# Output products started inside the merge stage, casts moved to ScalarE, wider bank rotation, short token tile last

## The chip, the cores and the metric

The kernel runs on one core of a Trainium2 chip. The metric is the device time in microseconds of one execution, the median of several runs. TensorE multiplies, VectorE and ScalarE do elementwise work, GpSimd (POOL in the profile) does a few fills, and SyncE (SP) issues the loads and stores.

## The reference

One inference step of a one-layer decoder, for a prompt of 512 tokens and 8 single-token samples, 520 tokens in all, model width 1024. What matters here is the end of the layer:

```
merged = (gates[:, :, 0] * einsum(o_nsa, w_br_nsa)
          + gates[:, :, 1] * einsum(o_gdn, w_br_gdn)
          + gates[:, :, 2] * einsum(o_mem, w_br_mem))
h = x + einsum('btd,de->bte', merged, w_out)
f = square(relu(einsum(rmsnorm(h, g_ffn), w_ff1)))
y = h + einsum('btf,fd->btd', f, w_ff2)
```

The gates are sigmoids of a projection of the normalized input. Everything is fp32.

## The kernel before

The program is six stages, each a block that all engines leave together. The last two are concerned: `stage_tail` (gates, branch projections, merge) and `stage_out_ffn` (output projection, norm, MLP). Between two stages local semaphores are cleared and all engines meet at a barrier.

**Precision.** Each fp32 operand x is split into a high part (a cast to fp32r) and a low part (x minus high), and each product is made of three matmuls per 128-row chunk: high x high, high x low, low x high (`product3`, L330). The cast is L299 and the subtraction L301, both in the helper `high_low` on VectorE, for weight tiles and activations alike. The low part is written over its source.

**Merge stage.** Weights come in tiles of 256 columns. The list `seq` alternates gate tiles (8 chunks, 24 matmuls a unit) and branch tiles (4 chunks, 12 matmuls a unit): gate 0, gate 1, then branch q and gate q + 2 for q = 0 to 11; the last two tiles are branches 10 and 11. A tile has four units: two blocks of 128 output columns times two halves of 260 tokens. TensorE writes gate units to banks 0 and 1 and branch units to banks 2, 3 and 4, and a branch unit waits until VectorE has taken the product three units back (`taken`). ScalarE makes the sigmoid (L2633). VectorE multiplies branch by gate (L2698), adds into `mergedT` (L2700) and, in the last third (branches 8 to 11, units 32 to 47), splits the finished unit into `mergedH` and the low part (L299, L301). The order on each engine is written out by `by_key`: small generators yield a due time, and the instruction with the lowest key is issued next. After `split(n)` of the next weight tile come the four units of a branch on VectorE; the last weight tile handled there, number 24, is the first tile of `w_out`.

**Output stage.** There are 20 output products, one for each of 5 token tiles (four of 128 rows, t = 0 to 3, and one of 8 rows, t = 4) and 4 column tiles n of `w_out`: first n = 0 for all t, then n = 1 for all t (products 0 to 9), then for each t in `order` n = 2 and n = 3 (10 to 19). Product u goes to bank 4 + u % 4 and waits, from u = 4 on, for the addition to h of product u - 4 (`h_ready`). h starts as x, loaded by SyncE at the start of the stage (2 MB, L2856). VectorE's order is: split of `w_out` tile 1 (`last_raw`), split of tile 2, five additions of n = 0, split of tile 3, five additions of n = 1, and so on. The loads of tiles 2 and 3 are also issued at the start of the stage. For each t in `order`, ScalarE sums squares (L2971), takes the root (L2980) and scales the rows (L2984), TensorE transposes them (`norm_turn`, L2901), and VectorE multiplies by the gain (L3010) and splits (`norm_keep`). The MLP's first unit needs the first three token tiles and its third unit needs all five. GpSimd fills `yT` with zeros once the last transposes are done (L2882). The MLP is four quarters of 32 units of 24 matmuls.

Of the kernel before, what the change touches and what calls it, by code (L numbers as in the profile page):

```python
# [169 lines left out]
class Kernel:  # L170
# [2238 lines left out]
    def tile_units(self):  # L2409

        return [(m, slice(HALF * h, HALF * h + HALF)) for m in range(WM) for h in range(2)]

    def out_tiles(self):
        return [[self.I["w_out"][:, a:a + WCOLS]] for a in range(0, DM, WCOLS)]

    def stage_tail(self):
# [67 lines left out]
        S = self.local_sem  # L2484
        gated, taken, added = (S("m_" + x) for x in ("gated", "taken", "added"))
        turned, oH_kept, oL_kept = (S("t_" + x) for x in ("turned", "oH_kept", "oL_kept"))
# [9 lines left out]
        with nc.Block() as block:  # L2496
# [44 lines left out]
            def _(pe):  # L2541
# [77 lines left out]

                by_key(dense(), turn(), sample())  # L2620

            @block.scalar
            def _(act):
                def dense():
                    for n, (kind, q) in enumerate(seq):
                        if kind == "gate":
                            for i, (m, tok) in enumerate(U):
                                yield unit_at(n, i + 1)
                                u = NU * q + i
                                act.wait_ge(acc, acc_of("gate", q, i))  # L2630
                                if q >= 2:
                                    act.wait_ge(taken, u - 2 * NU + 1)
                                act.activation(sig[:, q % 2, m, tok], ps[:, u % 2, 0:HALF], ACT.Sigmoid).then_inc(gated, 1)  # L2633
# [23 lines left out]

                by_key(dense(), turn(), sample())

            @block.vector  # L2660
            def _(dve):
                ch = Chain(S("s_chain"), dve)

                def split(n):
                    k, chunks = k0 + n, tiles[n][1]
                    dve.wait_ge(self.w_loaded[k % 2], self.loaded_at[k])
                    if n >= 2:
                        dve.wait_ge(acc, self.tile_end[k - 2])
                    cut = lambda x: x[:, 0:chunks, :]
                    self.high_low(dve, cut(raw[n % 3]), cut(self.wh[k % 2]), cut(low[n % 3]), self.w_high, k + 1).then_inc(self.w_split, 1)  # L2670

                def splits():
                    yield 0.1
                    split(0)
                    for n in range(1, NT_ + 1):
                        yield start[n - 1] + 0.2
                        split(n)

                def dense():
                    for n, (kind, q) in enumerate(seq):  # L2680
                        if kind == "gate":
                            continue
                        for i, (m, tok) in enumerate(U):
                            yield unit_at(n, i + 1) + 0.1
                            u = NU * q + i
                            dst, high, lo = (x[:, WM * (q % BP) + m, tok] for x in (self.mergedT, self.mergedH, self.mergedL))
                            dve.wait_ge(gated, u + 1)
                            dve.wait_ge(acc, acc_of("branch", q, i))
                            if u == 0:
                                dve.wait_ge(turned, EARLY)  # L2690
                            x, y = ps[:, 2 + u % 3, 0:HALF], sig[:, q % 2, m, tok]
                            if q < BP:
                                dve.tensor_tensor(dst, x, y, ALU.mult).then_inc(taken, 1)
                                continue
                            e = u - BP * NU
                            if e >= 2:
                                dve.wait_ge(added, e - 1)
                            dve.tensor_tensor(prod2[:, e % 2, :], x, y, ALU.mult).then_inc(taken, 1)  # L2698
                            dve.wait_ge(taken, u + 1)
                            dve.tensor_tensor(dst, dst, prod2[:, e % 2, :], ALU.add).then_inc(added, 1)  # L2700
                            if q >= 2 * BP:
                                dve.wait_ge(added, e + 1)
                                self.split_acts(dve, dst, high, lo)

# [97 lines left out]
    def stage_out_ffn(self):  # L2802
# [24 lines left out]
        acc, u0 = self.acc, self.units  # L2827
        order, UN, NO = (0, 1, 2, 4, 3), TT + 1, DM // WCOLS
        token = lambda t: slice(t * P, t * P + rows(t))
# [23 lines left out]
        with nc.Block() as block:  # L2853
# [31 lines left out]
            def _(pe):  # L2885
                def out_product(n, t):
                    u = index[n, t]
                    w = (self.wh[(base + n) % 2], wlow[(base + n) % 2]) if n < 2 else (woH[n - 2], woL[n - 2])
                    pe.wait_ge(self.w_split, base + n + 1)
                    if u >= 4:  # L2890
                        pe.wait_ge(h_ready, u - 3)
                    self.product3(pe, ps[0:rows(t), 4 + u % 4, 0:WCOLS], lambda i, c: X[i][:, c, token(t)], lambda i, c: w[i][:, c, :]).then_inc(acc, 1)

# [10 lines left out]
                for n in range(2):  # L2904
                    for t in range(UN):
                        out_product(n, t)
# [84 lines left out]
            def _(dve):  # L2991
# [6 lines left out]
                def add(n, t):  # L2998
                    R, u = rows(t), index[n, t]
                    hh = h[0:R, t, WCOLS * n:WCOLS * n + WCOLS]  # L3000
                    dve.wait_ge(acc, u0 + u + 1)
                    dve.tensor_tensor(hh, hh, ps[0:R, 4 + u % 4, 0:WCOLS], ALU.add).then_inc(h_ready, 1)  # L3002

# [16 lines left out]
                dve.wait_ge(h_in, 32)  # L3020
                for n in range(2):
                    split_out(n + 2)
                    for t in range(UN):
                        add(n, t)
                for k, t in enumerate(order):
# [97 lines left out]
```

## Time and profile before

| | |
|---|---|
| time, median of 3 runs | 1560.75 us (1556.61 to 1567.21) |
| profiled execution, its own time | 1570.02 us |
| its span | 1568.2 us |
| TensorE busy | 1434.7 us, 91% |
| VectorE busy | 865.2 us, 55% |
| ScalarE busy | 391.2 us, 25% |
| mean granted TensorE clock | 0.945 |

The span runs from the first to the last instruction; the execution's own time is 1.8 us longer. In the trace's rows a time is in microseconds from the start of the span, a matmul's own duration includes its passage through a pipeline, so the distance between starts is its cost, and the brackets at a row's end hold how long the engine was idle before it and what released it.

### The profile page before, as it was taken

The numbers are of one execution on the slowest core, as the hardware profiler recorded it, in microseconds if no ns is written. First come the engines' busy times: TensorE is split into PE (matmuls) and PEld (weight loads), VectorE is DVE, ScalarE is ACT, GpSimd is POOL, SyncE is SP. The second block draws the span as 40 slices with busy tenths as digits, with TensorE's granted clock in tenths as the row PEclk, the third lists the DMA queues.
The fourth block names the chain that finished last, engine by engine and source line by source line (L and its number), as shares of the span: only waits on it lengthen the run. The fifth ranks groups of instructions, "written<-read, shape, count | busy, mean of one in ns | idle before, by whom it ended". The sixth has DMA issues, their size and how long they took to land. (4 is left out here: it accounts for less than half of the span.)

```text
span 1568.2 us, 27050 instructions
## 1 busy us (share of the span) xinstructions
PE 1434.7 (91%) x11344; PEld 1322.1 (84%) x11344; DVE 865.2 (55%) x1576; ACT 391.2 (25%) x895; POOL 79.7 (5%) x74
## 2 busy tenths in 40 slices
PE   6999999999887887889667899999799999999998
PEld 5888889899877776768444798999799999999998
DVE  3556257877463665554524545545647647465563
ACT  3543032332352444443313410000021001010000
POOL 1000001100011111111000000000000000000000
PEclk8999999999988897979879899999999999999999
DMA  9132134222432000010666413332521232323221
GB/s 361 66 137 102 39 92 175 81 81 85 129 131 108 1 1 1 1 54 1 224 263 252 141 56 109 106 108 68 174 69 55 94 95 81 108 80 96 93 81 55
DMA packets 115648, 159.03 MB, mean 101 GB/s; under 512 B 6039, under 2 KB 106839, under 8 KB 112778
## 3 DMA queue, kind: packets, MB, share of 16 engines
q1 hardware_dynamic: 111886, 122.76, 24.5%
q0 software_dynamic: 2304, 33.56, 5.4%
q8 instruction: 84, 1.38, 0.4%
q10 hardware_dynamic: 1348, 1.12, 0.2%
q14 instruction: 26, 0.21, 0.0%
HBM read 145.04 MB, written 16.66 MB: 103 GB/s over the span
## 5 line engine op out<-in xcount | busy, mean ns | idle before, releaser
L330 PE MATMUL ps<-hH,wh 128*128 128x260 f32 x512 | 146.3, 286 | 2.6 <-DVE hT L301 2.6
L330 PE MATMUL ps<-hT,wh 128*128 128x260 f32 x512 | 146.0, 285 | 0.0
L330 PE MATMUL ps<-hH,wl 128*128 128x260 f32 x512 | 145.7, 285 | 0.0
L330 PE MATMUL ps<-mergedH,wh 128*128 128x260 f32 x512 | 145.7, 285 | 0.0
L330 PE MATMUL ps<-mergedT,wh 128*128 128x260 f32 x512 | 144.8, 283 | 0.0
L330 PE MATMUL ps<-mergedH,wl 128*128 128x260 f32 x512 | 144.5, 282 | 0.0
L330 PE MATMUL ps<-uH,wh 128*128 128x260 f32 x480 | 138.2, 288 | 0.0
L462 PE MATMUL ps<-XT,w 128*128 128x256 f32 (+1 forms) x512 | 124.3, 385 | 0.3 <-DVE hbias L615 0.3
L330 PE MATMUL ps<-uL,wh 128*128 128x260 f32 x384 | 109.4, 285 | 0.0
L330 PE MATMUL ps<-uH,tw 128*128 128x260 f32 x384 | 109.4, 285 | 0.0
L462 PEld LDWEIGHTS ps<-XT,w 128*128 128x128 f32 x512 | 93.0, 192 | 11.3 <-issue 0.9
L330 PEld LDWEIGHTS ps<-hH,wh 128*128 128x128 f32 x512 | 97.8, 191 | 2.9 <-DVE hT L301 2.8
L2988 ACT ACTIVATE positive<-ps 128x260 f32<-128x260 f32 x64 | 24.8, 388 | 302.3 <-PE ps L330 302.3
L330 PEld LDWEIGHTS ps<-hH,wl 128*128 128x128 f32 x512 | 97.9, 191 | 0.0
L330 PEld LDWEIGHTS ps<-hT,wh 128*128 128x128 f32 x512 | 97.6, 191 | 0.0
L330 PEld LDWEIGHTS ps<-mergedH,wl 128*128 128x128 f32 x512 | 96.7, 189 | 0.0
L330 PEld LDWEIGHTS ps<-mergedH,wh 128*128 128x128 f32 x512 | 96.3, 188 | 0.0
L330 PEld LDWEIGHTS ps<-mergedT,wh 128*128 128x128 f32 x512 | 96.3, 188 | 0.0
L330 PEld LDWEIGHTS ps<-uH,wh 128*128 128x128 f32 x480 | 91.5, 191 | 5.0 <-ACT sig L2633 3.0
L330 PE MATMUL ps<-wt,uH 128*128 128x256 f32 (+1 forms) x304 | 85.0, 280 | 0.0
L3077 DVE TENSOR_TENSOR yT<-yT,ps 128x260 f32<-128x260 f32 x64 | 27.1, 424 | 100.2 <-PE ps L330 100.2
L532 DVE COPY XT<-ps 64x256 f32<-64x256 f32 x128 | 53.2, 416 | 39.7 <-PE ps L450 38.4
(561 smaller groups left out, 3558.7 us busy)
## 6 DMA issues: line engine op xcount, KB each, us to landing
wt<-in_w_ff SPq DMA_DIRECT2D x32, 1024.0 KB, 5.4
wt<-in_w_in SPq DMA_DIRECT2D x15, 1024.0 KB, 5.4
tw<-in_w_in SPq DMA_DIRECT2D x12, 1024.0 KB, 5.2
ring<-in_cache_mem_kv SPq DMA_DIRECT2D x4, 2048.0 KB, 8.4
w<-in_cmp_w SPq DMA_DIRECT2D x8, 512.0 KB, 7.8
ring<-in_cache_win_kv SPq DMA_DIRECT2D x2, 2048.0 KB, 8.8
out_s_win<-in_cache_win_kv SPq DMA_DIRECT2D x1, 4088.0 KB
scratch_uhigh<-uH SPq DMA_DIRECT2D x1, 2080.0 KB
```

The lines of the kernel that those rows point to most:

```text
L330: ins = pe.matmul(out, lhsT(i, c), rhs(j, c), start=(first and c == 0 and k == 0), stop=(last and c == chunks - 1 and k == 2))
L462: return pe.matmul(out, self.w1[:, v, J * r + j, :], x, start=(i == 0), stop=(i == 2 * J - 1))
L532: ins = copy(slot(c)[e * HD:(e + 1) * HD, v, j:j + 2, g], ps[g * HD:(g + 1) * HD, u % 4, :].rearrange("p (j e n) -> p e j n", j=2, e=2)[:, e])
L2988: act.activation(positive[:, k % 4, :], ps[:, k % 4, 0:HALF], ACT.Relu).then_inc(relu, 1)
L3077: dve.tensor_tensor(y, y, ps[:, 4 + k % 4, 0:HALF], ALU.add).then_inc(summed, 1)
```

## The change

Five things, in two stages. (1) The first three output products (n = 0, t = 0, 1, 2) are issued by TensorE at the end of the merge stage, into banks 5, 6 and 7; for t = 0 and 1 the chunks are waited for one after the other (0 to 5, then 6, then 7). (2) In the last third of the merge stage the cast of each unit (`casts`) is done by ScalarE after the addition, and VectorE's subtraction (`lower`) follows one unit later. (3) The cast of the first `w_out` tile (`last_weight`) is done by ScalarE too, and VectorE only subtracts. (4) The output products rotate over six banks, 5, 6, 7, 4, 0, 1, for the first ten, and over 4 to 7 after that; VectorE does the additions of n = 0 before the split of `w_out` tile 2, and the split of tile 3 after the third addition of n = 1. (5) `order` is (0, 1, 2, 3, 4), so the 8-row tile is the last one instead of the fourth.

```
@@ -2410,6 +2410,12 @@
 
         return [(m, slice(HALF * h, HALF * h + HALF)) for m in range(WM) for h in range(2)]
 
+    OUT_EARLY, OUT_BANKS = 3, (5, 6, 7, 4, 0, 1)
+
+    def out_bank(self, u):
+
+        return self.OUT_BANKS[u % 6] if u < 2 * (TT + 1) else 4 + u % 4
+
     def out_tiles(self):
         return [[self.I["w_out"][:, a:a + WCOLS]] for a in range(0, DM, WCOLS)]
 
@@ -2482,7 +2488,9 @@
         turn_key = lambda i: 1.5 + 1.1 * i if i < EARLY else 47.0
 
         S = self.local_sem
-        gated, taken, added = (S("m_" + x) for x in ("gated", "taken", "added"))
+        gated, taken, added, cast = (S("m_" + x) for x in ("gated", "taken", "added", "cast"))
+        xs0, X3 = self.x_split.n, (self.mergedH, self.mergedL)
+        THIRD = 2 * BP * NU
         turned, oH_kept, oL_kept = (S("t_" + x) for x in ("turned", "oH_kept", "oL_kept"))
         back, summed = S("t_back"), S("t_summed")
         obr = proj[0:NB, 1:TT, C_KV:C_KV + NH * HD]
@@ -2618,9 +2626,39 @@
                         p.done(pe.matmul(ps[:, 6 + i % 2, :], rows_kv[:, 0, :], Vm[i % 2].rearrange("p c d -> p (c d)"), start=True, stop=True), f"add{i}", 0)
 
                 by_key(dense(), turn(), sample())
+                v.wait(pe, "add7", 0)
+                w = self.wh[(k0 + NT_) % 2], low[NT_ % 3]
+                for t in range(self.OUT_EARLY):
+                    pe.wait_ge(self.w_split, k0 + NT_ + 1)
+                    for c0, c1, units in ((0, 6, 11), (6, 7, 13), (7, KC, 15)):
+                        if t < 2:
+                            pe.wait_ge(self.x_split.sem, xs0 + 2 * units)
+                        else:
+                            pe.wait_ge(self.x_split.sem, xs0 + 2 * BP * NU)
+                        ins = self.product3(pe, ps[0:rows(t), self.OUT_BANKS[t], 0:W], lambda i, c: X3[i][:, c0 + c, t * P:t * P + rows(t)], lambda i, c: w[i][:, c0 + c, :],
+                                            c1 - c0, first=(c0 == 0), last=(c1 == KC))
+                    ins.then_inc(acc, 1)
 
             @block.scalar
             def _(act):
+                def last_weight():
+                    k = k0 + NT_
+                    yield start[NT_ - 1] + 0.2
+                    act.wait_ge(self.w_split, k)
+                    act.wait_ge(self.w_loaded[k % 2], self.loaded_at[k])
+                    act.wait_ge(acc, self.tile_end[k - 2])
+                    act.copy(self.wh[k % 2][:, :, :], raw[NT_ % 3][:, :, :]).then_inc(self.w_high, 1)
+
+                def casts():
+                    for n, (kind, q) in enumerate(seq):
+                        if kind == "gate" or q < 2 * BP:
+                            continue
+                        for i, (m, tok) in enumerate(U):
+                            yield unit_at(n, i + 1) + 0.5
+                            act.wait_ge(added, NU * (q - BP) + i + 1)
+                            at = WM * (q % BP) + m
+                            act.copy(self.mergedH[:, at, tok], self.mergedT[:, at, tok]).then_inc(cast, 1)
+
                 def dense():
                     for n, (kind, q) in enumerate(seq):
                         if kind == "gate":
@@ -2655,7 +2693,7 @@
                     v.wait(act, "so", 0)
                     a.done(act.activation(so, so, ACT.Sqrt), "ro", 0)
 
-                by_key(dense(), turn(), sample())
+                by_key(dense(), casts(), last_weight(), turn(), sample())
 
             @block.vector
             def _(dve):
@@ -2667,6 +2705,10 @@
                     if n >= 2:
                         dve.wait_ge(acc, self.tile_end[k - 2])
                     cut = lambda x: x[:, 0:chunks, :]
+                    if n == NT_:
+                        dve.wait_ge(self.w_high, k + 1)
+                        dve.tensor_tensor(low[n % 3][:, :, :], raw[n % 3][:, :, :], self.wh[k % 2][:, :, :].bitcast(F32), ALU.subtract).then_inc(self.w_split, 1)
+                        return
                     self.high_low(dve, cut(raw[n % 3]), cut(self.wh[k % 2]), cut(low[n % 3]), self.w_high, k + 1).then_inc(self.w_split, 1)
 
                 def splits():
@@ -2675,6 +2717,12 @@
                     for n in range(1, NT_ + 1):
                         yield start[n - 1] + 0.2
                         split(n)
+
+                def lower(u):
+                    q, (m, tok) = u // NU, U[u % NU]
+                    dve.wait_ge(cast, u - THIRD + 1)
+                    dst, high, lo = (x[:, WM * (q % BP) + m, tok] for x in (self.mergedT, self.mergedH, self.mergedL))
+                    self.x_split.inc(dve.tensor_tensor(lo, dst, high.bitcast(F32), ALU.subtract), 2)
 
                 def dense():
                     for n, (kind, q) in enumerate(seq):
@@ -2683,7 +2731,7 @@
                         for i, (m, tok) in enumerate(U):
                             yield unit_at(n, i + 1) + 0.1
                             u = NU * q + i
-                            dst, high, lo = (x[:, WM * (q % BP) + m, tok] for x in (self.mergedT, self.mergedH, self.mergedL))
+                            dst = self.mergedT[:, WM * (q % BP) + m, tok]
                             dve.wait_ge(gated, u + 1)
                             dve.wait_ge(acc, acc_of("branch", q, i))
                             if u == 0:
@@ -2698,9 +2746,10 @@
                             dve.tensor_tensor(prod2[:, e % 2, :], x, y, ALU.mult).then_inc(taken, 1)
                             dve.wait_ge(taken, u + 1)
                             dve.tensor_tensor(dst, dst, prod2[:, e % 2, :], ALU.add).then_inc(added, 1)
-                            if q >= 2 * BP:
-                                dve.wait_ge(added, e + 1)
-                                self.split_acts(dve, dst, high, lo)
+                            if u > THIRD:
+                                lower(u - 1)
+                    yield unit_at(NT_ - 1, NU) + 0.6
+                    lower(Q * NU - 1)
 
                 def turn():
                     for i, (br, t) in enumerate(turns):
@@ -2825,7 +2874,7 @@
         relu, squared, high, low, summed, turned, added, stored, zeroed = (
             S("ff_" + x) for x in ("relu", "squared", "high", "low", "summed", "turned", "added", "stored", "zeroed"))
         acc, u0 = self.acc, self.units
-        order, UN, NO = (0, 1, 2, 4, 3), TT + 1, DM // WCOLS
+        order, UN, NO = (0, 1, 2, 3, 4), TT + 1, DM // WCOLS
         token = lambda t: slice(t * P, t * P + rows(t))
         out_unit = [(n, t) for n in range(2) for t in range(UN)] + [(n, t) for t in order for n in (2, 3)]
         index = {x: u for u, x in enumerate(out_unit)}
@@ -2887,9 +2936,10 @@
                     u = index[n, t]
                     w = (self.wh[(base + n) % 2], wlow[(base + n) % 2]) if n < 2 else (woH[n - 2], woL[n - 2])
                     pe.wait_ge(self.w_split, base + n + 1)
-                    if u >= 4:
-                        pe.wait_ge(h_ready, u - 3)
-                    self.product3(pe, ps[0:rows(t), 4 + u % 4, 0:WCOLS], lambda i, c: X[i][:, c, token(t)], lambda i, c: w[i][:, c, :]).then_inc(acc, 1)
+                    earlier = [x for x in range(u) if self.out_bank(x) == self.out_bank(u)]
+                    if earlier:
+                        pe.wait_ge(h_ready, earlier[-1] + 1)
+                    self.product3(pe, ps[0:rows(t), self.out_bank(u), 0:WCOLS], lambda i, c: X[i][:, c, token(t)], lambda i, c: w[i][:, c, :]).then_inc(acc, 1)
 
                 def norm_turn(k):
                     R = rows(order[k])
@@ -2902,7 +2952,7 @@
                         ins.then_inc(n_turned, 1)
 
                 for n in range(2):
-                    for t in range(UN):
+                    for t in range(self.OUT_EARLY if n == 0 else 0, UN):
                         out_product(n, t)
                 for k, t in enumerate(order):
                     out_product(2, t)
@@ -2999,7 +3049,7 @@
                     R, u = rows(t), index[n, t]
                     hh = h[0:R, t, WCOLS * n:WCOLS * n + WCOLS]
                     dve.wait_ge(acc, u0 + u + 1)
-                    dve.tensor_tensor(hh, hh, ps[0:R, 4 + u % 4, 0:WCOLS], ALU.add).then_inc(h_ready, 1)
+                    dve.tensor_tensor(hh, hh, ps[0:R, self.out_bank(u), 0:WCOLS], ALU.add).then_inc(h_ready, 1)
 
                 def norm_keep(k):
                     t = order[k]
@@ -3018,10 +3068,13 @@
                 self.splits += 1
                 dve.memset(ss[:, :, :], 1.0).then_inc(mean, 1)
                 dve.wait_ge(h_in, 32)
-                for n in range(2):
-                    split_out(n + 2)
-                    for t in range(UN):
-                        add(n, t)
+                for t in range(UN):
+                    add(0, t)
+                split_out(2)
+                for t in range(UN):
+                    add(1, t)
+                    if t == 2:
+                        split_out(3)
                 for k, t in enumerate(order):
                     R = rows(t)
                     dve.wait_ge(squares, k + 1)
```

## Rows read from the trace of the kernel before

**Rows 1.** The page: its span and TensorE's busy time.

```profile
span 1568.2 us, 27050 instructions
PE 1434.7 (91%) x11344; PEld 1322.1 (84%) x11344; DVE 865.2 (55%) x1576; ACT 391.2 (25%) x895; POOL 79.7 (5%) x74
```

**Rows 2.** Chain that ended last, in time: start, us, what (matmuls counted).

```profile
1119.23 10.87 DMA wt<-in_w_out
...
1133.75 0.34 DVE h L3002
...
1134.23 28.46 PE ps L330 x240
...
1182.26 0.59 PE ps L2901 x8
...
1186.41 1.30 DVE hT L3010 x2
...
1187.74 3.27 DVE hH L299
...
1192.31 334.07 PE ps L330 x2760
```

**Rows 3.** Timeline of TensorE, matmuls that begin after an idle time.

```profile
1111.11 0.38 PE L330 MATMUL ps<-oH,wh 128*128 128x260 f32 x1 [2.20 <-DVE m_prod L2698]
...
1118.41 0.55 PE L330 MATMUL ps<-wh,mergedH 128*128 128x256 f32 x1 [5.60 <-PEq L222]
...
1134.23 0.28 PE L330 MATMUL ps<-wh,mergedH 128*8 128x256 f32 x1 [1.98 <-DVE h L3002]
...
1192.31 0.59 PE L330 MATMUL ps<-hH,wh 128*128 128x260 f32 x1 [2.62 <-DVE hT L301]
```

**Rows 4.** Windows: stretch, length, busy (instructions) per engine, granted clock, DMA, GB/s.

```profile
1118.00:1130.00 12.00, 11.59 (x79) 11.62 (x80) 3.54 (x3) 0.00 (x0) 0.00 (x0) 0.77 0.91 305
1192.00:1202.00 10.00, 9.70 (x57) 9.70 (x58) 7.39 (x13) 0.78 (x2) 0.00 (x0) 0.67 0.35 107
```

**Rows 5.** Timeline of VectorE at the end of the merge stage.

```profile
1067.83 0.42 DVE L2698 TENSOR_TENSOR m_prod<-ps,sig 128x260 f32<-128x260 f32 x1
...
1105.58 0.42 DVE L2698 TENSOR_TENSOR m_prod<-ps,sig 128x260 f32<-128x260 f32 x1
...
1106.50 0.30 DVE L299 CAST mergedH<-mergedT 128x260 fp32r<-128x260 f32 x1
1106.83 0.43 DVE L301 TENSOR_TENSOR mergedT<-mergedT,mergedH 128x260 fp32r<-128x260 f32 x1
1107.18 1.22 DVE L299 CAST wh<-tw 128x2048 fp32r<-128x2048 f32 x1
1108.43 2.29 DVE L301 TENSOR_TENSOR tw<-tw,wh 128x2048 fp32r<-128x2048 f32 x1
1110.64 0.42 DVE L2698 TENSOR_TENSOR m_prod<-ps,sig 128x260 f32<-128x260 f32 x1
...
1116.68 0.43 DVE L301 TENSOR_TENSOR mergedT<-mergedT,mergedH 128x260 fp32r<-128x260 f32 x1
```

**Rows 6.** Groups of ScalarE by line and form: count, busy us, mean ns.

```profile
L2640 ACT CAST oH<-ps 128x512 fp32r<-128x512 f32 x12 | 6.9, 585 | 15.8 <-PE ps L2581 15.7
...
L1269 ACT ACTIVATE graw<-graw 128x2048 f32<-128x2048 f32 x3 | 5.8, 1921 | 0.0
```

**Rows 7.** DMA view from 900 to 1200 us: loads, KB each, us from issue to landing.

```profile
tw<-in_w_out SPq DMA_DIRECT2D x2, 1024.0 KB, 5.1
```

**Rows 8.** Timeline of ScalarE: the first sigmoid of gate 10.

```profile
1072.93 0.39 ACT L2633 ACTIVATE sig<-ps 128x260 f32<-128x260 f32 x1 [8.26 <-PE ps L330]
```

**Rows 9.** The page's DMA issues: a load of 2 MB, us to landing.

```profile
ring<-in_cache_mem_kv SPq DMA_DIRECT2D x4, 2048.0 KB, 8.4
```

**Rows 10.** Timeline of VectorE: the cast of a norm tile.

```profile
1179.27 0.69 DVE L299 CAST hH<-hT 128x1024 fp32r<-128x1024 f32 x1
```

**Rows 11.** Timeline of GpSimd: the zero fill.

```profile
1186.88 3.57 POOL L2882 MEMSET yT<- 128x4160 f32 x1 [389.19 <-PE ps L2901]
```

## The prediction, made before the result was known

> **What bounds the kernel now.** The page comes first: TensorE is busy 91% of the span [rows 1], so a change pays where it fills TensorE's idle time, and work taken off the others pays only where TensorE waits for it. Next I read the chain that ended last, from the boundary of the last two stages on [rows 2]. The reader is to see that it is not TensorE there: it runs through the load of a w_out tile until 1130.10, the split and addition behind it until 1134.1, then TensorE without a break until 1182.26, a stretch of VectorE until 1192.3, and TensorE to the end. TensorE's timeline has the holes that belong to this [rows 3]: 2.20 us before the last branch unit, because VectorE had not yet taken product 44; 5.60 us at the boundary; 1.98 us before product 4; 2.62 us before the third MLP unit. Last come the windows [rows 4]: after the holes of 5.60 and 2.62 us the mean granted clock of the stretch is 0.77 and 0.67, a mix of the two levels 2.4 and 1.2 GHz, while no fall shows after 2.20 and 1.98 us.
>
> All of this is some 20 us of 1560, so the change is worth at most a little over 1%.
>
> **Part 1, the end of the merge stage.** VectorE's four operations for a unit take 1.60 us from 1105.58 to 1107.18; the cast takes the 0.33 us from 1106.50 to 1106.83 [rows 5]. Without it a unit takes 1.27 us. Before the last four units stands the split of tile 24: cast 1.25 us, subtraction 2.21 us to the next start [rows 5].
>
> In branch 10 the units 40 to 43 start at 1100.79 (1105.58 less three times 1.60). At 1.27 us each the last addition ends at 1105.5 and subtraction 42 at 1105.9. ScalarE casts units 40 to 42 in this time. Its price for 128x260 is not in the trace in this form. The bounds are 0.30 us (VectorE's own) and 0.585 us (a cast of 128x512) [rows 5, 6]; I take 0.38, between. Then comes tile 24, which waits for branch 10 to end, near 1104.5, and for its load: issued at 1098.9, when gate 11 had ended, it lands 5.1 us later, at 1104.0 [rows 7]. The nearest row for 128x2048 is 1.92 us [rows 6]; below it lies VectorE's 1.22 us [rows 5], above it four casts of 128x512, 2.34 us [rows 6]. I take 1.92: from 1104.7 to 1106.6, so VectorE idles 0.7 us and starts unit 44 at 1108.86, not 1110.64.
>
> TensorE's unit 47 waits for product 44 to be taken: 1109.3 instead of 1111.11, to 1110.8. Chunks 0 to 5 of output product 0 are ready (subtraction 42, 1105.9) and take 18 x 0.1186 = 2.1 us (28.46 us for 240 matmuls [rows 2]). Chunk 6 needs subtraction 44, done at 1111.5. Chunk 7 needs subtraction 46: units 45 to 47 follow at 1.27 us, and subtraction 46 ends at 1114.0. So TensorE waits 0.8 us, until 1114.05. Products 1 and 2 take 2.85 us each (24 x 0.1186), the last subtraction (1114.4) is in time for product 2, and TensorE is done at 1120.2.
>
> The moved casts queue ahead of sigmoids on ScalarE, with gate 10 and gate 11 behind them. Branch 8 starts on VectorE at 1067.83 [rows 5], its last addition ends 3 x 1.27 + 0.9 later at 1072.5, the cast at 1073.0, and the sigmoid that ran at 1072.93 [rows 8] is 0.1 us late. TensorE needs that bank two units later, about 2.9 us on. Cost nothing; beyond some 2.5 us of delay it would be paid one for one.
>
> **Part 2, the boundary.** VectorE's last operation ended at 1117.11 (1116.68 + 0.43) [rows 5] and TensorE began at 1118.41 [rows 3]: 1.30 us. Now TensorE is the last to arrive, 1120.2. The trace has no such boundary with TensorE last at this place; I take the same 1.30, so the stage starts at 1121.5, 3.1 us later than before. SyncE's loads of h and of w_out tiles 2 and 3 move by the same 3.1 us.
>
> **Part 3, products 3 to 19.** Banks 4, 0 and 1 are free, so products 3, 4 and 5 need only weights: tile 1 is split 3.5 us after the start (1.22 + 2.29 [rows 5]), before product 5 at 1127.2. Product 6 reuses bank 5 and waits for the addition of product 0, hence for h. Nothing in the trace waits for h alone. The bounds: it can be there before product 6 asks, at 1130.0, or take as long as the w_out load behind it, 10.87 us [rows 2], until 1132.4. The row of equal size (2 MB) lands after 8.4 us [rows 9]; from 1121.5 that is 1129.9, and 0.6 us of additions and signals make 1130.5. Stall 0.5 us, between 0 and 2.9.
>
> Tile 2 lands at 1133.2 and is split by 1136.8, tile 3 by 1141.5, behind three additions; products 10 and 11 need them at 1141.9 and 1144.7. So the wait for the load, which was on the path, is covered by ten products instead of four.
>
> From product 4's start at 1134.23 the old kernel needs 48.03 us until the transposes at 1182.26 [rows 2], for 16 products and three transposes. The new one has 17 from 1121.5: 48.03 + 2.85 + 0.5 = 51.4, which ends at 1172.9. **Gain 9.4 us**, at full clock.
>
> **Part 4, the end of the norm.** I stay on the old times, as if products ended at 1182.26. The last scaling on ScalarE is as long for 8 rows as for 128, so the last transposes still end near 1186.5. VectorE has the 128-row tile to finish first (1.30 of gain multiplication from 1184.0, 0.7 cast, 1.2 subtraction, to 1187.3). Then comes the 8-row tile, whose cast meets the zero fill. In the old kernel the 128x1024 cast took 3.27 us [rows 2] against 0.69 elsewhere [rows 10], and the fill ran from 1186.88 to 1190.45 [rows 11]. Two readings fit: the cast is stretched 4.7 times, or it waits until the fill is over and then takes its 0.69, which gives 1191.1 against an observed 1191.0. I take the second. The 8-row cast then ends at 1190.7, its subtraction at 1190.95, and the third MLP unit starts at 1191.0 instead of 1192.31: 1.3 us. The hole shrinks from 2.62 to about 1.3 us, under the 1.98 us that was not followed by a fall. The fall cost: 57 matmuls in 9.69 us where 0.12 us each (334.07/2760 [rows 2]) would make 81, so 24 x 0.12 = 2.9 us. **Gain 4.2 us**; bounds 0 (fall stays, wait as long) and 5.6.
>
> The Trainium skill has a rule on this, in "SBUF — State Buffer", section "SBUF: two separate sides": VectorE in a two-port mode and GpSimd take one pair of ports under a lock held for the whole instruction, and the loser waits. This case's trace agrees, 3.27 us for a 0.69 us cast. By that rule the sum is 13.6 us; by a shared bandwidth the 8-row cast would take 0.9 us instead, the hole would close, and the sum would be 15.0. The page adds that an operation with two SBUF inputs is held up only by a GpSimd operation that reads SBUF; no run here shows that yet.
>
> **The sum.** 9.4 + 4.2 = 13.6 us. Span 1554.6, own time of a profiled run 1556.4. The profiled execution lies 9.3 us above the median of the runs shown; against the median the forecast is 1560.75 - 13.6 = **1547.2 us**.
>
> **The rivals.**
> *The clock falls at the boundary.* For: a hole of 0.8 us, then one of 1.3 us, within 8 us. Against: 1.98 and 2.20 us alone did no harm [rows 3]. Its price is as after 1118.41: 79 matmuls in 11.6 us where 0.1186 each would make 98, so 2.2 us, formerly hidden under the wait for product 4, now paid. With the MLP fall staying as well, 2.9 more. Times 1549.4 and 1552.3. Chance 0.23.
> *The load of h takes the place of the old wait.* At 10.87 us product 6 stalls 2.9 instead of 0.5 us: 1549.6. For: three loads are in flight together. Against: h is issued first. Chance 0.10.
> *The early products don't run early.* If chunk 7's wait in effect held back all of product 0 (casts late, VectorE's queue late), product 0 starts near 1114.4 instead of 1110.8 and no longer waits 0.8 us inside: 2.8 us lost, 1550.0. Against: subtraction 42 leads by 5 us. Chance 0.05.
> *The zero fill only stretches* (or doesn't meet) the 8-row cast: 15.0 us, 1545.8. Chance 0.07.
> *Slower than before.* The clock falls at the boundary and stays at the lower level. At half the clock a matmul of 0.1186 us costs at most 0.1186 more, so the gain of 13.6 is gone after 115 matmuls, some five products; for all 17 products, 408 matmuls, it is 48.4 us: 1595.6. Against: both stretches with a fall [rows 4] have a mean clock well above half, so each fall ended inside its 12 or 10 us. Chance 0.03.
>
> **How the numbers follow.** The forecast has 0.50, the cases above 0.48, and 0.02 is for what I don't see. The likeliest case's own range is 1545 to 1550. Three runs of the same kernel lie 10.6 us apart, so a median can be some 4 us off. The range goes from 1545 less 4 to 1552.3 plus 5: 1541 to 1557. One per cent of 1560.75 is 15.6 us, about what a measurement of this kernel can tell from no change; the bound is at 1545.1. The forecast and its milder rivals fall within it, and by scatter or a slightly larger gain about a quarter of the chance falls beyond it: faster 0.25, same 0.72, slower 0.03.
>
> **What the new profile would show.** Right: ScalarE rows with a cast of 128x2048 near 1.9 us, 36 matmuls and more of product 0 to 2 before the boundary, a boundary hole of 1.3 us, no chain through w_out's load, TensorE unbroken from there to the transposes save a hole under 1 us before product 6, a VectorE cast of 128x64 of over 2 us beside the fill, and a granted clock of 1.00 in the MLP's first units. Wrong: rows with half clock after the boundary (part 3 too large), a hole over 2 us before product 6 (part 3), a sigmoid that delays a gate unit (part 1), or a fall in the MLP's first ten microseconds (part 4).

## The result, and the profile after

The changed kernel took 1553.9 us (median of 6 runs, 1549.6 to 1557.42), the kernel before 1564.59 us in the runs beside it (6 runs, the three of before among them). The ratio is 0.9938, 95% interval 0.9915 to 0.9960, so 10.7 us by the medians, less than one per cent. Forecast were 1547.2 us, a range of 1541 to 1557, and 13.6 us. Of the 6.7 us between the forecast and the median, 3.8 are the kernel before, whose median is 1564.59 in these six runs and was 1560.75 in the three shown, and 2.9 are the gain. The profiled execution has a span of 1555.6 us against 1568.2, 12.6 us less.

The page of the profile after, its span and busy times, beside [rows 1]:

```profile
span 1555.6 us, 27068 instructions
PE 1430.7 (92%) x11344; PEld 1317.2 (85%) x11344; DVE 857.2 (55%) x1559; ACT 399.0 (26%) x912; POOL 80.5 (5%) x74
```

VectorE lost 8 us and ScalarE gained 8. The chain that ended last (start us, us, what), where [rows 2] has the old one:

```profile
1122.44 8.65 DMA h<-in_x_sample
1131.11 0.43 DVE h L3052
1131.68 22.90 PE ps L330 x192
...
1179.37 2.83 DVE hH L299
1182.51 331.28 PE ps L330 x2760
```

The load at the head of the chain is another one: h, not a w_out tile. The last piece has the same 2760 matmuls in 331.28 us instead of 334.07. TensorE's matmuls behind an idle time, to hold against [rows 3]:

```profile
1110.34 0.39 PE L330 MATMUL ps<-oH,wh 128*128 128x260 f32 x1 [0.52 <-DVE m_prod L2746]
...
1114.68 0.38 PE L330 MATMUL ps<-wh,mergedH 128*128 128x256 f32 x1 [0.17 <-DVE mergedT L2725]
...
1122.07 0.35 PE L330 MATMUL ps<-wh,mergedH 128*128 128x256 f32 x1 [1.09 <-PEq L222]
...
1131.68 0.35 PE L330 MATMUL ps<-wh,mergedH 128*128 128x256 f32 x1 [0.92 <-DVE h L3052]
...
1182.51 0.39 PE L330 MATMUL ps<-hH,wh 128*128 128x260 f32 x1 [0.93 <-DVE hT L301]
```

Where there were holes of 2.20, 5.60, 1.98 and 2.62 us there are now 0.52, 1.09, 0.92 and 0.93, and one of 0.17 inside the first output product, where it waits for chunk 7. The windows of the same two places, against [rows 4], show no half clock:

```profile
1120.00:1132.00 12.00, 9.99 (x84) 8.95 (x83) 4.43 (x6) 0.00 (x0) 0.00 (x0) 1.00 0.74 259
...
1182.00:1192.00 10.00, 9.49 (x79) 9.50 (x80) 9.54 (x18) 1.17 (x4) 0.14 (x1) 1.00 0.34 106
```

Stages ahead of the change begin and end at other times in each execution, so all that follows is counted from one event behind them, the start of the last gate sigmoid, which all kernels have (row L2633 before, L2671 after). Before:

```profile
1098.85 0.39 ACT L2633 ACTIVATE sig<-ps 128x260 f32<-128x260 f32 x1 [2.49 <-PE ps L330]
```

and after:

```profile
1099.75 0.39 ACT L2671 ACTIVATE sig<-ps 128x260 f32<-128x260 f32 x1 [2.49 <-PE ps L330]
```

From there to the end of the span are 469.35 us before (1568.2 - 1098.85) and 455.85 us after (1555.6 - 1099.75). In this pair of traces the changed part gave 13.50 us. I call this length the measure. The forecast was 13.6. So the question for the experiments was not only which part gave what, but why the timed medians show 10.7.

### The profile page after: what moved, and what is told of

Its sections match the earlier page's. It is cut to its first block and busy times, and to the rows that moved or that the text cites. A ratio compares the mean times of both kernels' runs of the same rounds, so it can differ in the third digit from the quotient of the medians.

```text
span 1555.6 us, 27068 instructions
## 1 busy us (share of the span) xinstructions
PE 1430.7 (92%) x11344; PEld 1317.2 (85%) x11344; DVE 857.2 (55%) x1559; ACT 399.0 (26%) x912; POOL 80.5 (5%) x74
## 5 line engine op out<-in xcount | busy, mean ns | idle before, releaser
L462 PEld LDWEIGHTS ps<-XT,w 128*128 128x128 f32 x512 | 93.0, 192 | 11.3 <-issue 0.9
```

The source lines that it names most:

```text
L462: return pe.matmul(out, self.w1[:, v, J * r + j, :], x, start=(i == 0), stop=(i == 2 * J - 1))
```

## The experiments

All numbers are from one profile each unless a ratio is given. The timed ratios of the changed kernel and of the variants that undo one of its parts run from 0.9927 to 0.9952, with intervals that all overlap, so the parts are told apart by the profiles and not by the times. "Third unit" is the start of the third MLP unit, in us after the last gate sigmoid.

| kernel | first product behind the boundary | third unit | third unit to end | measure |
|---|---|---|---|---|
| before | 19.56 | 93.46 | 375.89 | 469.35 |
| before, second profile | 19.55 | 93.02 | 374.60 | 467.62 |
| before, third | 19.55 | 92.84 | 374.73 | 467.57 |
| before, fourth | 19.55 | 93.15 | 374.41 | 467.56 |
| before + part 4 | 19.57 | 91.58 | 373.09 | 464.67 |
| before + part 5 | 19.55 | 91.46 | 373.15 | 464.61 |
| changed | 22.32 | 82.76 | 373.09 | 455.85 |
| changed, second profile | 22.32 | 82.68 | 373.09 | 455.77 |
| changed, old order | 22.32 | 84.74 | 374.62 | 459.36 |
| changed, no early product | 16.82 | 86.95 | 373.10 | 460.05 |
| changed, casts on VectorE | 24.10 | 84.84 | 373.15 | 457.99 |
| changed, one early product | 16.82 | 81.78 | 373.19 | 454.97 |
| changed, late fill | 22.31 | no hole | | 454.75 |
| changed, late fill, h in two loads | 22.32 | no hole | | 453.55 |

### The old order in the changed kernel

```
-        order, UN, NO = (0, 1, 2, 3, 4), TT + 1, DM // WCOLS
+        order, UN, NO = (0, 1, 2, 4, 3), TT + 1, DM // WCOLS
```

> The changed kernel with part 5 undone (order 0, 1, 2, 4, 3). Measure: from the start of the last gate sigmoid to the end of the span, 469.35 us before and 455.85 us changed. Theory 1 (the short hole is what keeps the clock up): the hole before the third MLP unit grows from 0.9 to about 2.6 us and the clock falls after it, so the measure is 1.3 to 1.8 us longer for the hole and 2.8 for the clock, 460.2. Rival (the fall is chance, not the hole): 457.4 with a granted clock of 1.00 behind a hole of 2.6 us.

The measure is 459.36, between the two theories. The third unit is 1.98 us later, of which 0.30 was already there before product 6 (32.23 against 31.93, a longer wait for the load of h, which the order does not touch), so the order is worth 1.68 us of hole. Behind the hole of 2.62 us the clock fell, but for half as long as in the trace of before: from the third unit to the end 1.5 us more than the changed kernel's 373.09, not 2.8. A hole of the same length did not bring the same fall. The timed ratio is 0.9929 (0.9895 to 0.9964), which does not tell it from the changed kernel.

### No early product

```
-    OUT_EARLY, OUT_BANKS = 3, (5, 6, 7, 4, 0, 1)
+    OUT_EARLY, OUT_BANKS = 0, (5, 6, 7, 4, 0, 1)
```

> The changed kernel with no output product in the merge stage. Same measure, 455.85 us changed. The boundary hole becomes 4.6 us instead of 1.1, the load of h starts 5.7 us earlier and no product waits for it. Theory 1: product 6 starts 1.8 us later than now and a clock fall after the boundary adds 2.2: 459.9. Rival (the hole is all): 457.7 with the clock at 1.00. Third reading (early products were the change's main gain): over 462.

Theory 1 holds, 460.05 for 459.9. TensorE's timeline behind the boundary, and the window there:

```profile
1115.77 0.55 PE L330 MATMUL ps<-wh,mergedH 128*128 128x256 f32 x1 [4.53 <-PEq L222]
```

```profile
1115.00:1127.00 12.00, 11.23 (x75) 11.26 (x76) 4.43 (x6) 0.00 (x0) 0.00 (x0) 0.75 0.86 290
```

The three early products are worth 4.2 us, and about half of that is the clock that stays up: 75 matmuls in 11.2 us where 0.1186 us each would make 95, so 2.3 us. The kernel with one early product, below, gives the same figure by another way: its boundary comes at 16.82 us too, without a fall, and its third unit is 5.17 us sooner (81.78 against 86.95), 2.85 for the one product and 2.3 for the clock. Ratio to before 0.9945 (0.9918 to 0.9972).

### Casts back on VectorE

```
-                by_key(dense(), casts(), last_weight(), turn(), sample())
+                by_key(dense(), turn(), sample())
...
-                    if n == NT_:
-                        dve.wait_ge(self.w_high, k + 1)
-                        dve.tensor_tensor(low[n % 3][:, :, :], raw[n % 3][:, :, :], self.wh[k % 2][:, :, :].bitcast(F32), ALU.subtract).then_inc(self.w_split, 1)
-                        return
...
-                            if u > THIRD:
-                                lower(u - 1)
-                    yield unit_at(NT_ - 1, NU) + 0.6
-                    lower(Q * NU - 1)
+                            if q >= 2 * BP:
+                                dve.wait_ge(added, e + 1)
+                                high, lo = (x[:, WM * (q % BP) + m, tok] for x in (self.mergedH, self.mergedL))
+                                self.split_acts(dve, dst, high, lo)
```

> The changed kernel with parts 2 and 3 undone: VectorE casts again, the early products stay. Theory 1: the last branch unit starts near 1.6 us later, chunk 7 is ready 1.7 us later, and all behind it moves by as much: 457.6. Rival (casts hide in the wait for h, since the load of h is what product 6 waits for): 455.9 to 456.3. Against the rival: the load starts at the boundary, which moves too.

457.99, as theory 1 has it. The last branch unit waits 2.20 us again, the boundary comes 1.78 us later (24.10 against 22.32), and the load of h moves with it, so nothing hides it. The rest of the 2.14 us is a wait for h of 1.20 us instead of 0.92; in the other three profiles with three early products and h in one load the same wait was 0.84, 0.99 and 1.22 us, so I put 1.8 us down to the casts and 0.3 to the scatter of the load. Ratio 0.9952 (0.9926 to 0.9977).

### Part 4 alone

```
...
-                    if u >= 4:
-                        pe.wait_ge(h_ready, u - 3)
+                    earlier = [x for x in range(u) if self.out_bank(x) == self.out_bank(u)]
+                    if earlier:
+                        pe.wait_ge(h_ready, earlier[-1] + 1)
...
-                for n in range(2):
-                    split_out(n + 2)
-                    for t in range(UN):
-                        add(n, t)
+                for t in range(UN):
+                    add(0, t)
+                split_out(2)
+                for t in range(UN):
+                    add(1, t)
+                    if t == 2:
+                        split_out(3)
```

(`out_bank` and the six banks are those of the change.)

> The kernel before with part 4 alone: six banks and the additions of n = 0 ahead of the split of tile 2. Theory 1: the 1.98 us wait behind the load goes, but the half clock after the boundary, which that wait used to hide, is now paid: 469.35 - 4.4 + 2.2 = 467.1. Rival (the wait for the load was the largest single term): 464.9 or less.

The third unit starts at 91.58, 1.88 us sooner than in the first profile of before, where theory 1 has 2.2, and 1.3 to 1.6 us sooner than in the other three (next section). But the measure is 464.67, the rival's number, for a reason that neither had. The row of the third unit and the window behind it:

```profile
1188.61 0.39 PE L330 MATMUL ps<-hH,wh 128*128 128x260 f32 x1 [2.62 <-DVE hT L301]
```

```profile
1188.00:1198.00 10.00, 9.39 (x78) 9.40 (x79) 9.66 (x17) 1.16 (x3) 0.00 (x0) 1.00 0.35 107
```

The hole of 2.62 us is there as before, and no fall follows it. The timed ratio, 0.9991 (0.9959 to 1.0022), does not tell part 4 alone from no change.

### The kernel before again, three times

No edit.

> The kernel before, unchanged, for a second profile. From the last gate sigmoid to the end of the span the first one had 469.35 us, 2.8 of them in a half-clock stretch behind the 2.62 us hole. If the hole brings the fall each time: 469.4, with some 27 matmuls 0.21 us apart behind it. If the fall is chance (the kernels with the old order showed 27, 16 and 1 such matmuls): anything from 466.5 to 469.4. The half-clock stretch behind the 5.60 us hole is expected each time by both.

> The same once more, a third profile of the kernel before: 469.4 if the fall always follows, 466.5 to 469.4 if it is chance.

> The same once more, a fourth profile of the kernel before: 469.4 if the fall always follows, 466.5 to 469.4 if it is chance.

The measure is 467.62, 467.57 and 467.56. The windows behind the 2.62 us hole, one from each profile:

```profile
1179.00:1189.00 10.00, 9.90 (x70) 9.91 (x71) 8.51 (x16) 0.78 (x2) 0.00 (x0) 0.83 0.37 107
```

```profile
1188.00:1198.00 10.00, 9.93 (x70) 9.93 (x71) 8.49 (x16) 0.78 (x2) 0.00 (x0) 0.83 0.38 107
```

```profile
1193.00:1203.00 10.00, 9.31 (x66) 9.31 (x67) 8.70 (x16) 0.78 (x2) 0.00 (x0) 0.83 0.38 107
```

A fall each time, at 0.83 and not 0.67: 1.3 to 1.6 us from the third unit to the end, where the first profile had 2.8. The first profile of before held the dearest fall of all six with that hole (2.8, 1.5, 1.6, 1.3; 1.5 in the changed kernel with the old order; none with part 4 alone). Against the median of the four, 467.6, the change gave 11.8 us in the measure. That is a ratio of 0.9925, inside the interval of the first timing and of the second one below.

The clock is not all of the difference. Product 4 waits for the load of the w_out tile behind h, which landed 10.87 us after its issue in the first profile and 10.44, 10.26 and 10.57 us in the other three; the hole before product 4 was 1.98 us there and 1.30, 1.31 and 1.75 here. The row of the third profile:

```profile
1130.00 0.28 PE L330 MATMUL ps<-wh,mergedH 128*8 128x256 f32 x1 [1.31 <-DVE h L3002]
```

So the first profile was long by 0.3 to 0.6 us in this load, besides the 1.2 to 1.5 us of the clock.

### Part 5 alone

```
-        order, UN, NO = (0, 1, 2, 4, 3), TT + 1, DM // WCOLS
+        order, UN, NO = (0, 1, 2, 3, 4), TT + 1, DM // WCOLS
```

> The kernel before with part 5 alone, the 8-row tile last. Theory 1: the third MLP unit starts 1.7 to 2.0 us sooner after the last transposes and no fall follows the hole of 0.93 us, so 466.6 less 1.9 = 464.7 us. Rival (the gain of part 5 shows only with the banks changed): 466.6.

464.61 for 464.7. From product 4 to the third unit are 56.39 us against 58.08 before: 1.69 us less, the hole of 0.93 for 2.62 us, as in the changed kernel, and a clock of 1.00 behind it. (Product 4 itself came 0.3 us sooner than in the first profile of before, by the scatter of the load just described.)

### The fill moved away from the cast

```
                 pool.wait_ge(n_turned, 2 * UN)
+                pool.wait_ge(acc, f0 + 6)
                 pool.memset(yT[:, :, :], 0.0).then_inc(zeroed, 1)
...
+                                if k == 0:
+                                    dve.wait_ge(zeroed, 1)
```

(the second wait stands before VectorE's first addition to `yT` and replaces the one before the quarters)

> The changed kernel with GpSimd's zero fill moved behind the sixth MLP unit, so that it no longer meets the 8-row cast. Theory 1 (the cast waits for the fill's end): the 128x64 cast takes 0.20 us instead of 2.82, its tile is ready before the second MLP unit ends, and the hole of 0.93 us before the third unit closes; some later cast of VectorE is held for up to 3.6 us, at no cost, since TensorE is units ahead of needing it. From the last gate sigmoid to the end 455.85 - 0.9 = 454.9. Rival (the cast was slow for another reason, its place behind the large tile): it stays at 2.8 us and the hole stays.

In the changed kernel VectorE's timeline at the 8-row tile, and GpSimd's fill:

```profile
1177.91 1.23 DVE L301 TENSOR_TENSOR hT<-hT,hH 128x1024 fp32r<-128x1024 f32 x1
1179.05 0.28 DVE L3060 TENSOR_TENSOR hT<-ps,gcol 128x32 f32<-128x32 f32 x2
1179.37 2.82 DVE L299 CAST hH<-hT 128x64 fp32r<-128x64 f32 x1
```

```profile
1178.56 3.58 POOL L2931 MEMSET yT<- 128x4160 f32 x1 [379.83 <-PE ps L2951]
```

With the fill moved, the same cast, and then the one that meets the fill:

```profile
1173.65 0.20 DVE L299 CAST hH<-hT 128x64 fp32r<-128x64 f32 x1
...
1188.29 2.94 DVE L299 CAST mergedH<-mergedT 128x260 fp32r<-128x260 f32 x1
```

```profile
1187.50 3.58 POOL L2932 MEMSET yT<- 128x4160 f32 x1 [391.69 <-PE ps L330]
```

Theory 1 holds. The 8-row cast takes 0.20 us, the hole before the third unit is gone, and the measure is 454.75, 1.1 us less than 455.85. The fill now holds a cast in the MLP, 2.94 us for 0.29, and TensorE shows no idle time for it. The held casts end 0.05 and 0.15 us after the fill (1182.19 against 1182.14, 1191.23 against 1191.08), and the 0.69 us cast of the kernel before ended 0.56 us after it (1191.01 against 1190.45, [rows 2] and [rows 11]). In all three the end is that of the fill plus the cast's own time, less 0.13 to 0.15 us. Fill and cast touch different tiles, the rows show the cast as running and not as waiting for a signal, and with the fill moved it is another cast that is slow, the one that the fill now meets.

### One early product

```
-    OUT_EARLY, OUT_BANKS = 3, (5, 6, 7, 4, 0, 1)
+    OUT_EARLY, OUT_BANKS = 1, (5, 6, 7, 4, 0, 1)
```

> The changed kernel with one output product in the merge stage instead of three. The load of h then starts 5.7 us earlier, and product 6 comes 5 products behind the boundary instead of 3. Theory 1 (the three early products only move work across the boundary; what pays is that the boundary comes under work, and h's load binds with three): the wait of 0.92 us before product 6 goes, nothing else changes: 454.9. Rival (each early product pays for itself): one to three microseconds longer than 455.85.

454.97 for 454.9. The boundary hole is 1.27 us where it was 1.09 with three, the wait before product 6 is gone, the clock stays:

```profile
1100.95 0.35 PE L330 MATMUL ps<-wh,mergedH 128*128 128x256 f32 x1 [1.27 <-PEq L222]
```

Two of the three early products pay nothing here, and they delay the load that becomes the next wait, 0.9 us by the measure. Ratio 0.9927 (0.9900 to 0.9955).

### Both waits taken out

```
-                sp.dma_start(h[:, 0:TT, :], I["x_prompt"][0].rearrange("(t p) d -> p t d", p=P)).then_inc(h_in, 16)
-                sp.dma_start(h[0:NB, TT, :], I["x_sample"][:, 0, :]).then_inc(h_in, 16)
+                xp = I["x_prompt"][0].rearrange("(t p) d -> p t d", p=P)
+                sp.dma_start(h[:, 0:TT, 0:WCOLS], xp[:, :, 0:WCOLS]).then_inc(h_first, 16)
+                sp.dma_start(h[0:NB, TT, :], I["x_sample"][:, 0, :]).then_inc(h_first, 16)
+                sp.dma_start(h[:, 0:TT, WCOLS:DM], xp[:, :, WCOLS:DM]).then_inc(h_in, 16)
```

with the late fill; the additions of n = 0 wait for `h_first`, those of n = 1 for `h_in` as well.

> The changed kernel with the fill late and the load of h cut so that the 256 columns of n = 0 come first. Theory 1: both remaining waits go, 0.9 and 1.0 us: from the last gate sigmoid to the end 453.9, and 0.1% by the times, near what five rounds can tell. Rival (the wait behind the boundary is the w_out loads, which the extra transfer doesn't speed up): 454.9.

453.55, a little under theory 1. VectorE's additions of n = 0 now start 4.1 us behind the boundary (1123.55, boundary at 1119.47), not 9.0:

```profile
1123.55 1.42 DVE L3055 TENSOR_TENSOR h<-h,ps 128x256 f32<-128x256 f32 x4 [0.50 <-DMA h<-in_x_sample]
```

By the times: 1548.54 us against 1563.16 of before beside it, ratio 0.9900 (0.9883 to 0.9917). The changed kernel had 1552.68 us and 0.9934 (0.9917 to 0.9951) beside the same runs of before. The intervals just touch, and the measures are 2.2 us apart, so it is most likely the faster of the two.

### The changed kernel again

No edit.

> The changed kernel once more, with more rounds and a second profile. If its gain is as in the first pair of traces, 13.5 us from the last gate sigmoid to the end, the ratio to before is 0.9914. If 2.8 us of that were the clock's chance fall after the 2.62 us hole of the one trace of before, and the other executions of before had it seldom, the ratio is 0.993. In its trace the clock stays at 1.00 behind the 0.93 us hole by both.

The measure is 455.77, within 0.1 us of the first. The clock is 1.00 behind both holes. The ratio is 0.9934 (0.9917 to 0.9951), nearer to the reading in which the fall of 2.8 us was seldom. The four profiles of before make this more exact: a fall came each time, of 2.8 us once and of 1.3 to 1.6 three times. Its span was 1542.1 us where the first had 1555.6: all of that difference lies ahead of the change, since the last gate sigmoid came at 1086.33 instead of 1099.75.

## Why the prediction was right, point by point

**The bound.** TensorE's holes were the right thing to count. Nearly every one changed as forecast. The third MLP unit was forecast at 82.75 us after the last gate sigmoid (1191.0 less the 9.4 of part 3, less 1098.85), and it came at 82.76. That the two agree so closely is luck: the transposes forecast for 1172.9 (74.05 us after the sigmoid) came 0.4 us later, and the hole behind them closed by 0.4 us more than forecast. The measure's 13.50 us for a forecast 13.6 is no proof of the size either, since the sum was read from the same trace of before, with its dear fall and its slow load.

**Part 1.** ScalarE's 128x260 cast was 0.41 us (forecast 0.38), its 128x2048 cast 1.91 (1.92):

```profile
1105.09 0.41 ACT L2660 CAST mergedH<-mergedT 128x260 fp32r<-128x260 f32 x1 [0.93 <-DVE mergedT L2748]
1105.62 1.91 ACT L2650 CAST wh<-tw 128x2048 fp32r<-128x2048 f32 x1
```

VectorE's unit fell to 1.14 us, below the forecast 1.27:

```profile
1111.12 0.42 DVE L2746 TENSOR_TENSOR m_prod<-ps,sig 128x260 f32<-128x260 f32 x1
...
1112.26 0.42 DVE L2746 TENSOR_TENSOR m_prod<-ps,sig 128x260 f32<-128x260 f32 x1
```

I had subtracted the cast's own distance only; the subtraction now starts 0.35 us after the start of the addition, where the cast had started 0.47 after it. So the wait for chunk 7 was shorter than the 0.8 us forecast, 0.17 of idle time in the row of product 0. The sigmoids cost nothing, as forecast: in both traces TensorE has no idle time of over 0.1 us in the 60 us before the last gate sigmoid. What the casts are worth was not in the forecast as a sum of its own. Undoing them costs 2.1 us, of which 1.8 are theirs; the forecast had unit 47 start 1.8 us sooner (1109.3 instead of 1111.11).

**Part 2.** The first product behind the boundary came at 22.32 us after the sigmoid for a forecast 22.65, the hole was 1.09 us for 1.30.

**Part 3.** The wait for w_out went, and the load of h took its place, as the second rival said. It landed 9.07 us after its issue (1131.09 - 1122.02), between the 8.4 and 10.87 of the bounds; the wait was 0.92 us for a forecast 0.5. The rival was right in kind and wrong in size: 0.4 us, not 2.4. The term of 9.4 us came out at 9.0 (93.46 - 82.76 = 10.70, less the 1.69 of the order). Against the other three profiles of before it is 8.4 to 8.7.

**The rival of a clock fall at the boundary** did not come about. In seven profiles of kernels with early products the hole of 1.1 to 1.3 us was followed by none; without early products, at 4.53 us, it came. No trace shows a lasting fall.

**Part 4.** The 8-row cast waited for the end of the fill, and the stretch by shared bandwidth is ruled out: a 0.20 us cast took 2.82 us where 4.7 times its own time would be 0.9, and a 0.29 us cast 2.94, both until the fill ended. That is the lock of the Trainium skill, "SBUF — State Buffer", section "SBUF: two separate sides". The page's other half, that an operation with two SBUF inputs is not held by a fill, agrees with a row too: the subtraction at 1177.91 kept its 1.23 us although the fill began within it, at 1178.56. VectorE came first here, so a lock would have held the fill; the fill took 3.58 us, and 3.57 in the kernel before, where it met no such subtraction. One row is not proof. The hole gave 1.7 us for a forecast 1.3.

**The term that was mis-sized** is the 2.9 us for the clock's fall in part 4. It was right for the trace it was read from (331.28 against 334.07). But it was put into the sum as a property of the hole, and of the kernel before. Five other profiles with a hole of 2.62 us gave 1.6, 1.5, 1.5, 1.3 and 0. With 1.5, the middle of the six, the forecast would have been 12.2 us, ratio 0.9922, which both intervals hold; 13.6 us is 0.9913, just outside both. The stated bounds of part 4, 0 to 5.6 us, did hold it.

**How the parts add up.** With each undone in the changed kernel: early products 4.2 us, order 3.5 (of which 0.3 is h's arrival and 1.5 the clock), casts 2.1 (of which 0.3 is h's arrival). The bank rotation and VectorE's order were not undone in the changed kernel; alone, on the old kernel, they brought the third unit forward by 1.9 us against the first profile of before and by 1.5 against the middle of the four. The latter makes 11.3 of the 11.8 us against the median profile. In the first pair 1.3 us of the dear fall and 0.4 of the slow load come on top, which makes 13.0 of 13.5. The 0.5 that is left I don't assign; parts measured one at a time in two kernels need not add up.

## What to carry to other kernels

Work moved across a barrier pays only as far as it covers what the engine would otherwise wait for: one early product did all that three did, and the further two delayed the loads behind the barrier. When a wait behind a load is removed, look up what else was issued with that load; it is next in line. A price that comes from a clock fall in one trace is a chance, not a term: profile the kernel before more than once, or put it into the range alone.

## What the runs showed of the hardware that I had not expected

The same 2.62 us hole was followed by 2.8, 1.6, 1.5, 1.5, 1.3 and 0 us of lost time in six profiles; four of these, 2.8, 1.6, 1.5 and 1.3, are of one unchanged kernel. The granted clock of the 10 us behind it was 0.67, 0.83 four times, and 1.00. Holes of 0.93 us were followed by none in six profiles, holes of 4.53 and 5.6 us by one in all seven. Of the holes between, 1.30 to 1.98 us before product 4 (five profiles) were followed by none. What decides how long a fall behind the 2.62 us hole lasts, no run here shows.

The length of everything ahead of the change scattered far more than the change is worth: the last gate sigmoid came between 1084.13 and 1100.54 us in the profiles, while the stretch from there to the end repeated to 0.1 us in the two profiles of the changed kernel, where the clock did not fall (455.85 and 455.77).
